# Norm sums with tokens on the partitions, and value products one step later

## The chip, the cores and the metric

The kernel runs on one core of a Trainium2 chip. The metric is the device time of one execution, in microseconds. The engines of a core are TensorE (PE), VectorE (DVE), ScalarE (ACT), GpSimd (POOL) and SyncE (SP), which issues the transfers from memory. They run side by side and wait for each other on semaphores.

## The reference

Two layers of a transformer block work on 256 latent tokens and 256 context tokens of width 1024, in fp32. A layer is a SwiGLU half step, four parallel token mixers (A: differential attention, B: neighbourhood attention, C and D: grouped attention, D with a window and a sink) merged by gates and an output projection, and a second SwiGLU half step. Each of these three sub-layers j = 0, 1, 2 is wrapped the same way:

```
u = rms_norm(h, g_in) * (1 + scale) + shift
y = sublayer(u)
h = h + gate * rms_norm(y, g_out)      # rms_norm(x) = x * rsqrt(mean(x*x) + 1e-6) * g
```

So between two sub-layers there is a seam: the mean square of y over the 1024 features of each token gives the factor r, h becomes h + r\*y, and the mean square of the new h gives the factor R of the next norm. In layer 1 the context tokens are dropped after the mixers' keys and values, so the last seam has 256 tokens and the others 512.

## The kernel before

Features stand on the 128 partitions, in KT = 8 tiles, and tokens on the free axis (T = 512 or 256). PSUM is a tile `ps` of 8 banks of 512 columns. Every large fp32 product is done in three parts: high of the weights by high of the activations (L338), high by low (L339), and low by high (L347). `split_high` (ScalarE, L321) and `split_low` (VectorE, L327) make the two halves of each weight unit, two units ahead.

The order of work is written out by hand for each engine; each stage adds its instructions to every engine's queue in turn. The stages of a sub-layer are `Norm`, then `Hidden` and `Down` or the four `Branch` stages, `Merge` and `Out`. `Down` and `Out` are `Result` stages: for each of the 8 tiles of y, `take` (ScalarE) squares the product, copies it with its gain and squares the scaled value, and `add` (VectorE) sums these and h\*y over the tiles into `ssq`, `energy` and `cross`.

The seam. The mean square of the new h isn't computed from h but from sums that are ready earlier: sum(h\*h) + 2 r sum(h\*y) + r\*r sum(y\*y), with the gain in y. `Norm.tensor` sums `ssq` with the last `sq`, `energy` and `cross` over the partitions by products with a matrix of ones (L558 to L564). With ones as the 128 columns of weights each result stands on all partitions: 128x512 numbers of which every row is the same. Then `root` takes a logarithm and an exponential over 512 columns (L507, L509) for r; VectorE makes the sum above in four wide steps on `ssq` and `power` (L613, L617, L620, L622), with `scale_y(0)` between them; a second `root` gives R. From there a loop over the 8 tiles runs: `tmp` = h\*R (L635), ScalarE applies scale and shift (L582) and makes `u_high` (L586), VectorE makes `u_low` (L608), and adds r\*y to h for the tile after (L600, L604). `Norm.head` on TensorE follows tile by tile with the first six weight units (L649, 96 products). The first norm of the program has no result before it: `statistics` squares h on ScalarE and `sums` (L548) adds on TensorE, amid the modulation products (L373, L390) of the first stage.

The branches. A `Branch` walks over J steps (16 in layer 0, 8 in layer 1), each for 128 queries of a pair of heads: scores (L1155), maximum, exponential, scaling (L1499), `flip` transposes the probabilities (L1165), `keep_probs` copies them to `pt` (L1314), and after two steps `mix(p)` multiplies with the values (L1180); `high_of_out` (L1327) and `low_of_out` (L1505) take the result out. Between these stand the products of gates and of the next branch's projections, spread over points of the steps. In B, C and D `mix` writes one bank, so `mix(p)` waits for `o_done` of the pair before, set by `low_of_out`; the last one, `mix(NP - 1)`, follows the last `flip` after the loop:

```
for j in range(J):
    ... scores(j + early), window_parts(1 + 2 * j)
    if j % 2 == 0 and j:
        mix(j // 2 - 1)
    flip(j)
    self.window_parts(pe, 2 + 2 * j)
mix(NP - 1)
```

Of the kernel before, what the change touches and what calls it, by code (L numbers as in the profile page):

```python
# [23 lines left out]
P = 128  # L24
D = 1024
# [157 lines left out]
def build(nc, tokens, small, cond, weights, mods, na_rows, h_kept, c_kept, out, stop=None):  # L183
# [3 lines left out]
    with ExitStack() as ctx:  # L187
# [26 lines left out]
        rstd = place("rstd", [2, S_ALL], F32, at)  # L214
        ssq = place("ssq", [S_ALL], F32, at + 4 * KB)
# [8 lines left out]
        power = place("power", [S_ALL], F32, at); at += 2 * KB  # L224
# [159 lines left out]
        def mod_turn(pe, g):  # L384

            pe.wait_ge(mod_copied.sem, g + 1)
            if g:
                pe.wait_ge(mod_added.sem, g)
            for c in range(2):
                t = pe.matmul(ps[:, 5, 8 * c:8 * (c + 1)], mod_row[:, c * P:(c + 1) * P], sm("pick"),  # L390
                              start=c == 0, stop=c == 1, skip_group_check=True)
            t.then_inc(mod_turned.sem, 1)

        def mod_add(dve, g):
            dve.wait_ge(mod_turned.sem, g + 1)
            tiles = slice(KT * MOD_ORDER[g], KT * (MOD_ORDER[g] + 1))
            dve.tensor_tensor(mod[:, tiles].rearrange("p (j c) s -> p c j s", c=2), ps[:, 5, 0:2 * KT].rearrange("p (c j s) -> p c j s", c=2, s=2),
# [114 lines left out]
        class Norm(Stage):  # L512
# [3 lines left out]
            def __init__(self, layer, j, T, result):  # L516
# [6 lines left out]
                self.y_root = signals.new("y_rstd", 2 if result else 0)  # L523
                self.power_steps = signals.new("power_steps", 4 if result else 1)
                self.h_root = signals.new("h_rstd", 2)
                self.y_scaled = signals.new("y_scaled", KT if result else 0)
# [4 lines left out]
                self.ready = signals.new("u_ready", KT)  # L531

            def statistics(self, act):
# [7 lines left out]
                root(act, ps[:, 7, 0:T], rstd[:, 1, 0:T], self.h_root, 1.0 / D)  # L541

            def sums(self, pe):
                for k in range(KT):
                    pe.wait_ge(self.squared.sem, self.squared.at(k + 1))
                    if k == 0:
                        pe.wait_ge(ones_set.sem, ones_set.at(1))
                    pe.matmul(ps[:, 7, 0:self.T], ones[:, :], sq[:, k % 2, 0:self.T], start=k == 0, stop=k == KT - 1)\  # L548
                        .then_inc(self.summed.sem, 1)

            def tensor(self, pe):
                if not self.result:
                    return
                r, T = self.result, self.T
                if (self.l, self.j) in ((0, 1), (1, 0)):
                    pe.wait_ge(mod_done.sem, (MOD_UNITS - MOD_FIRST * KT) // (2 if self.l == 0 else 1))
                pe.wait_ge(r.squares.sem, r.squares.at(KT - 1))
                pe.matmul(ps[:, 7, 0:T], ones[:, :], ssq[:, 0:T], start=True, stop=False)  # L558
                pe.wait_ge(r.squared.sem, r.squared.at(KT))
                pe.matmul(ps[:, 7, 0:T], ones[:, :], sq[:, 1, 0:T], start=False, stop=True).then_inc(self.summed.sem, 1)  # L560
                pe.wait_ge(r.energies.sem, r.energies.at(KT))
                pe.matmul(ps[:, 2, 0:T], ones[:, :], energy[:, 0:T], start=True, stop=True).then_inc(self.summed.sem, 1)
                pe.wait_ge(r.crosses.sem, r.crosses.at(KT - 1))
                pe.matmul(ps[:, 3, 0:T], ones[:, :], cross[:, 0:T], start=True, stop=True).then_inc(self.summed.sem, 1)  # L564

            def scalar(self, act):
                T = self.T
                if self.result:
                    act.wait_ge(self.summed.sem, self.summed.at(1))
                    root(act, ps[:, 7, 0:T], rstd[:, 0, 0:T], self.y_root, 1.0 / D)  # L570
                for n in range(self.n0 + AHEAD, self.n0 + HEAD - 2):
                    split_high(act, n)
                if self.result:
                    act.wait_ge(self.power_steps.sem, self.power_steps.at(4))
                    root(act, power[:, 0:T], rstd[:, 1, 0:T], self.h_root, 1.0 / D)
# [14 lines left out]
            def vector(self, dve):  # L590
                T = self.T
# [5 lines left out]
                r, R, steps = rstd[:, 0, 0:T], rstd[:, 1, 0:T], self.power_steps  # L597
# [12 lines left out]
                if self.result:  # L610
                    dve.wait_ge(self.y_root.sem, self.y_root.at(2))
                    dve.wait_ge(self.summed.sem, self.summed.at(2))
                    dve.tensor_tensor(ssq[:, 0:T], ps[:, 2, 0:T], r, ALU.mult).then_inc(steps.sem, 1)  # L613
                    scale_y(0)
                    dve.wait_ge(self.summed.sem, self.summed.at(3))
                    dve.wait_ge(steps.sem, steps.at(1))
                    dve.scalar_tensor_tensor(out=ssq[:, 0:T], in0=ps[:, 3, 0:T], scalar=2.0, in1=ssq[:, 0:T],  # L617
                                             op0=ALU.mult, op1=ALU.add).then_inc(steps.sem, 1)
                    dve.wait_ge(steps.sem, steps.at(2))
                    dve.tensor_tensor(ssq[:, 0:T], ssq[:, 0:T], r, ALU.mult).then_inc(steps.sem, 1)  # L620
                    dve.wait_ge(steps.sem, steps.at(3))
                    dve.tensor_tensor(power[:, 0:T], power[:, 0:T], ssq[:, 0:T], ALU.add).then_inc(steps.sem, 1)  # L622
# [3 lines left out]
                else:  # L626
                    dve.wait_ge(self.summed.sem, self.summed.at(KT))
                    dve.tensor_copy(power[:, 0:T], ps[:, 7, 0:T]).then_inc(steps.sem, 1)
                dve.wait_ge(self.h_root.sem, self.h_root.at(2))
# [122 lines left out]
        class Result(Stage):  # L752
# [4 lines left out]
            def result_signals(self, layer, j):  # L757
# [10 lines left out]
                self.crosses = signals.new("h_times_y_added", crossed and KT - 1)  # L768
# [31 lines left out]
            def add(self, dve, m, b):  # L800
# [17 lines left out]
                dve.tensor_tensor(energy[:, 0:T], energy[:, 0:T], sq_y[:, b, 0:T], ALU.add).then_inc(self.energies.sem, 1)  # L818
                dve.wait_ge(self.crossed.sem, self.crossed.at(m + 1))
                if past(m - 1):  # L820
                    dve.wait_ge(self.crosses.sem, self.crosses.at(m - 1))
                dve.tensor_tensor(cross[:, 0:T], cross[:, 0:T], hy[:, b, 0:T], ALU.add).then_inc(self.crosses.sem, 1)

        class Down(Result):
# [11 lines left out]
            def tensor(self, pe):  # L836
                def two_rows(i, last):
                    for e, unit in enumerate(self.units):
# [8 lines left out]
                        product(pe, n, n0, [(ps[:, r, 0:self.T], [(w, k0 + w) for w in range(DOWN_K[part])])],  # L847
# [73 lines left out]
        class Branch(Stage):  # L921
# [194 lines left out]
            def tensor(self, pe):  # L1116
# [77 lines left out]
                for j in range(J):  # L1194
# [5 lines left out]
                    if j % 2 == 0 and j:  # L1200
                        mix(j // 2 - 1)
# [683 lines left out]
```

## Time and profile before

| | |
|---|---|
| time, median of 3 runs | 2534.37 us (2529.94 to 2536.66) |
| the profiled execution's own time | 2532.3 us |
| its span in the profile | 2530.5 us |
| TensorE busy | 2428.9 us (96%) |
| VectorE busy | 1581.3 us (62%) |
| ScalarE busy | 1064.8 us (42%) |
| mean granted TensorE clock | 0.988 of 2.4 GHz |

The span goes from the first to the last instruction; the time also holds what lies around it. In the rows, times are microseconds and durations of single instructions nanoseconds where a row says mean ns. `<-` after an idle time names what the engine waited for. PEld is the load of weights on TensorE. An fp32 product shows as two passes (x2).

### The profile page before, as it was taken

The page shows a single profiled execution, that of the slowest core. Times are in us where ns is not written, and L with a number is a line of the kernel's source. Part 1 is how long each engine was busy: PE and PEld are TensorE (multiplying, and loading weights), DVE is VectorE, ACT ScalarE, POOL GpSimd, SP SyncE. Part 2 cuts the span into 40 slices and gives each one's busy share as a digit, 9 for nine tenths or more (in the row PEclk, how much of TensorE's full clock was granted, in tenths as well). Part 3 has the DMA queues.
Part 4 walks back from the last instruction along what each step waited for, and adds up shares of the span by engine and source line. Part 5 has one row for each costly group of instructions (what it writes and reads, how often), then busy time and mean ns, then how long its engine had stood idle before and what let it go on. Part 6 is the DMA issues. An engine that isn't in the chain of part 4 may idle for free.

```text
span 2530.5 us, 31850 instructions
## 1 busy us (share of the span) xinstructions
PE 2428.9 (96%) x12584; PEld 1973.4 (78%) x12584; DVE 1581.3 (62%) x2620; ACT 1064.8 (42%) x1842; POOL 27.4 (1%) x43
## 2 busy tenths in 40 slices
PE   6999998999999999989999989999989999988998
PEld 3888886877767676768888868888868788778998
DVE  2798888355455557688887874333355456588654
ACT  5222235355454535462222342222354555556444
POOL 0000000000000000000000000000000000000000
PEclk9999999999999999999999999999999999999999
DMA  5556554321322112225655523322234243233554
GB/s 234 184 207 216 187 178 159 95 76 63 104 71 71 63 67 84 71 88 192 210 206 191 186 99 108 100 99 85 96 113 141 76 142 121 88 125 126 185 178 154
DMA packets 98069, 331.42 MB, mean 131 GB/s; under 512 B 11009, under 2 KB 12033, under 8 KB 97281
## 3 DMA queue, kind: packets, MB, share of 16 engines
q1 hardware_dynamic: 97922, 329.39, 38.4%
q8 instruction: 100, 1.64, 0.3%
q14 instruction: 47, 0.39, 0.0%
HBM read 323.06 MB, written 6.29 MB: 130 GB/s over the span
## 4 chain that ended last, share of the span: by engine, by line
PE 90%; DVE 4%; ACT 3%; issue 1%; DMA 1%; SPq 0%; POOL 0%; DVEq 0%; ACTq 0%
PE ps L347 26%; PE ps L338 24%; PE ps L339 24%; PE ps L649 5%; PE ps L1180 3%; PE ps L1155 3%; PE ps L1165 3%; DVE w_low L327 1%; ACT w_high L321 1%; ACT prob L1304 0%; PE ps L548 0%; DMA mod_first<-in_mods 0%; DVE stat L1464 0%; PE ps L1124 0%; ACT pt L1314 0%
## 5 line engine op out<-in xcount | busy, mean ns | idle before, releaser
L327 DVE TENSOR_TENSOR w_low<-raw,w_high 128x1024 fp32r<-128x1024 f32 (+1 forms) x488 | 551.7, 1136 | 495.3 <-ACT w_high L321 494.5
L321 ACT ACTIVATE w_high<-raw 128x1024 fp32r<-128x1024 f32 (+1 forms) x488 | 481.6, 990 | 762.1 <-DMA raw<-in_weights 761.9
L338 PE MATMUL ps<-u_high,w_high 128*128 128x512 f32 (+1 forms) x2208 | 771.0, 361 | 4.2 <-DVE acc L1421 1.4
L339 PE MATMUL ps<-u_low,w_high 128*128 128x512 f32 (+1 forms) x2208 | 762.6, 357 | 0.0
L347 PE MATMUL ps<-u_high,w_low 128*128 128x512 f32 (+1 forms) x2496 | 542.9, 362 | 4.8 <-DVE w_low L327 4.8
L347 PEld LDWEIGHTS ps<-u_high,w_low 128*128 128x128 f32 x2496 | 422.5, 190 | 91.6 <-issue 19.7
L338 PEld LDWEIGHTS ps<-u_high,w_high 128*128 128x128 f32 x2208 | 418.8, 190 | 89.4 <-issue 17.1
L339 PEld LDWEIGHTS ps<-u_low,w_high 128*128 128x128 f32 x2208 | 418.9, 190 | 58.1
L410 DVE CUSTOM_DVE_ANT_0 ps<-mod_raw,c_all,smalls 128x1024 f32<-128x1024 f32 x256 | 319.5, 1290 | 2.2 <-DMA mod_raw<-in_mods 1.7
L338 PE MATMUL ps<-hid_high,w_high 128*128 128x512 f32 (+1 forms) x704 | 249.0, 362 | 0.0
L339 PE MATMUL ps<-hid_low,w_high 128*128 128x512 f32 (+1 forms) x704 | 249.0, 362 | 0.0
L347 PE MATMUL ps<-hid_high,w_low 128*128 128x512 f32 (+1 forms) x704 | 161.6, 362 | 0.0
L338 PEld LDWEIGHTS ps<-hid_high,w_high 128*128 128x128 f32 x704 | 132.9, 189 | 20.6
L339 PEld LDWEIGHTS ps<-hid_low,w_high 128*128 128x128 f32 x704 | 132.9, 189 | 20.6
L1304 ACT ACTIVATE prob<-ps,stat 128x512 f32<-128x512 f32 (+1 forms) x192 | 116.5, 616 | 54.3 <-DVE stat L1475 54.3
L347 PEld LDWEIGHTS ps<-hid_high,w_low 128*128 128x128 f32 x704 | 122.5, 189 | 20.6
L1314 ACT ACTIVATE pt<-ps 128x1024 f32<-128x1024 f32 (+2 forms) x96 | 76.3, 795 | 145.0 <-PE ps L1165 144.7
L1464 DVE TENSOR_REDUCE stat<-ps 128x2 f32<-128x1024 f32 (+1 forms) x96 | 100.4, 1046 | 45.2 <-PE ps L1155 43.1
L649 PE MATMUL ps<-u_high,w_high 128*128 128x512 f32 (+1 forms) x288 | 89.7, 398 | 37.6 <-ACT u_high L586 37.6
L743 DVE TENSOR_TENSOR hid<-silu_g,ps 128x512 f32<-128x512 f32 (+1 forms) x88 | 54.4, 618 | 98.5 <-PE ps L347 98.2
L1155 PE MATMUL ps<-k_all,q_all 64*128 64x512 f32 (+1 forms) x384 | 93.7, 570 | 6.6 <-ACT prob L1304 6.4
L649 PEld LDWEIGHTS ps<-u_high,w_high 128*128 128x128 f32 x288 | 56.5, 205 | 51.3 <-issue 41.3
(151 smaller groups left out, 2258.5 us busy)
## 6 DMA issues: line engine op xcount, KB each, us to landing
raw<-in_weights SPq DMA_DIRECT2D x360, 512.0 KB, 3.5
mod_raw<-in_mods SPq DMA_DIRECT2D x128, 512.0 KB, 4.2
raw<-in_weights SPq DMA_DIRECT2D x64, 384.0 KB, 3.1
raw<-in_weights SPq DMA_DIRECT2D x64, 320.0 KB, 2.9
mod_first<-in_mods SPq DMA_DIRECT2D x16, 512.0 KB, 13.1
h_kept<-h SPq DMA_DIRECT2D x16, 256.0 KB, 2.0
na_bias<-in_na_rows SPq DMA_DIRECT2D x16, 256.0 KB, 4.0
h<-h_kept SPq DMA_DIRECT2D x2, 2048.0 KB, 8.0
```

The source lines that it names most:

```text
L321: act.activation(w_high[s][:, 0:width], raw[s][:, 0:width], ACT.Copy).then_inc(high_made.sem, 1)
L327: dve.tensor_tensor(w_low[s][:, 0:width], raw[s][:, 0:width], w_high[s][:, 0:width], ALU.subtract).then_inc(low_made.sem, 1)
L338: pe.matmul(o, w_high[s][:, w], x_high(x), start=first and a == 0, stop=False)
L339: pe.matmul(o, w_high[s][:, w], x_low(x), start=False, stop=False)
L347: done = pe.matmul(o, w_low[s][:, w], x_high(x), start=False, stop=last and a == len(terms) - 1)
L410: done = dve.tensor_tensor_reduce(out=ps[:, 4 + 2 * s:6 + 2 * s].rearrange("p a b -> p (a b)"), in0=mod_raw[i % MOD_SLOTS][:, :], in1=c_al ...
L649: pe.matmul(ps[:, banks[e], 0:W], w_high[SLOT_OF[self.n0 + e]][:, k], x[:, k, 0:W], start=k == 0 and x is u_high, stop=False)
L1155: m = pe.matmul(ps[:, self.score_bank(j) + s, 0:nkeys], q_all[rows, t, q:q + P], k_all[rows, kt, key:key + nkeys], start=True, stop=True)
L1165: m = pe.transpose(ps[:, 2 + s, c * P:(c + 1) * P], prob[:, j % 2, s, c * P:(c + 1) * P], ident)
L1304: e = act.activation(prob[:, j % 2, s, 0:nkeys], ps[:, self.score_bank(j) + s, 0:nkeys], ACT.Exp, bias=stat[:, j % 2, 1, s:s + 1], scale=S ...
L1314: act.activation(pt[:, j // 2 % 2, 0:ns, 0:nkeys // P, half], ps[:, 2:2 + ns, 0:nkeys].rearrange("p s (c q) -> p s c q", q=P), ACT.Copy).t ...
L1464: dve.tensor_reduce(stat[:, j % 2, 0], both[:, :, 0:nkeys], AX.X, ALU.max).then_inc(self.maxed.sem, 1)
```

## The change

1. The sums of a seam are turned. The sums' data are now the weights, 128 tokens at a time, and one column of ones moves, so that a result is one number per token, tokens on the partitions: 128x4 numbers instead of 128x512 (128x2 for 256 tokens). Each sum is four products (two for 256 tokens).
2. `ssq` and `cross` without their last tile are summed by `early_sums`, before the last low products of the `Result` stage; the last `sq` and `hy` are added in `Norm.tensor`; VectorE no longer adds the last `hy` to `cross`.
3. Both roots and the four steps of the sum work on 128x4 numbers in `by_token`; `small_root` replaces `root`; a third exponential gives sqrt of the mean square, so that the energy is combined in another form.
4. To bring r and R back to all partitions, ScalarE scales the unit matrix per token block (`on_diagonal`, an activation of 128x128 with a per-partition scale), and TensorE multiplies ones by it (`spread_out`). r and R then stand in PSUM banks 4 and 5, and VectorE reads them there.
5. Only one of two `split_high` stands ahead of the second root, the other behind it.
6. The first norm does the same; its `spread_out` stands in TensorE's queue behind the sums. The modulation's turned rows move from bank 5 to bank 3.
7. In B, C and D `mix(p)` runs at step 2p + 3 instead of 2p + 2, with its copies on ScalarE and VectorE; A and the last pair stay where they are.

```diff
+            def on_diagonal(self, act, which, row, signal):
+                for c in range(self.T // P):
+                    act.activation(diag[:, which, c], ident, ACT.Copy, scale=by_token[:, row, c:c + 1]).then_inc(signal.sem, 1)
+            def spread_out(self, pe, which, signal):
+                for c in range(self.T // P):
+                    pe.wait_ge(signal.sem, signal.at(c + 1))
+                    done = pe.matmul(ps[:, 4 + which, c * P:(c + 1) * P], ones[:, :], diag[:, which, c], start=True, stop=True)
+                done.then_inc(self.spread.sem, 1)
+            def small_root(self, act, of, row, steps):
+                act.activation(by_token[:, row, 0:self.T // P], of, ACT.Ln, scale=1.0 / D, bias=eps[:, 0:1]).then_inc(steps.sem, 1)
+                act.wait_ge(steps.sem, steps.at(1))
+                act.activation(by_token[:, row + 1, 0:self.T // P], by_token[:, row, 0:self.T // P], ACT.Exp, scale=-0.5).then_inc(steps.sem, 1)
...
             def sums(self, pe):
-                    pe.matmul(ps[:, 7, 0:self.T], ones[:, :], sq[:, k % 2, 0:self.T], start=k == 0, stop=k == KT - 1)\
-                        .then_inc(self.summed.sem, 1)
+                    for c in range(self.T // P):
+                        done = pe.matmul(ps[:, 2, c:c + 1], sq[:, k % 2, c * P:(c + 1) * P], ones[:, 0:1], start=k == 0 and c == 0,
+                                         stop=k == KT - 1 and c == self.T // P - 1, skip_group_check=True)
+                    done.then_inc(self.summed.sem, 1)
+                self.spread_out(pe, 1, self.h_diag)
...
             def tensor(self, pe):
+                pe.wait_ge(r.squared.sem, r.squared.at(KT))
+                r.sums_of(pe, sq[:, 1], 2, False, True).then_inc(self.summed.sem, 1)
+                pe.wait_ge(r.crossed.sem, r.crossed.at(KT))
+                r.sums_of(pe, hy[:, 1], 3, False, True).then_inc(self.summed.sem, 1)
...
-                pe.matmul(ps[:, 7, 0:T], ones[:, :], ssq[:, 0:T], start=True, stop=False)
-                pe.wait_ge(r.squared.sem, r.squared.at(KT))
-                pe.matmul(ps[:, 7, 0:T], ones[:, :], sq[:, 1, 0:T], start=False, stop=True).then_inc(self.summed.sem, 1)
                 pe.wait_ge(r.energies.sem, r.energies.at(KT))
-                pe.matmul(ps[:, 2, 0:T], ones[:, :], energy[:, 0:T], start=True, stop=True).then_inc(self.summed.sem, 1)
-                pe.wait_ge(r.crosses.sem, r.crosses.at(KT - 1))
-                pe.matmul(ps[:, 3, 0:T], ones[:, :], cross[:, 0:T], start=True, stop=True).then_inc(self.summed.sem, 1)
+                r.sums_of(pe, energy, 7, True, True).then_inc(self.summed.sem, 1)
+                self.spread_out(pe, 0, self.y_diag)
+                self.spread_out(pe, 1, self.h_diag)
...
+            def sums_of(self, pe, x, bank, first, last):
+                for c in range(self.T // P):
+                    done = pe.matmul(ps[:, bank, c:c + 1], x[:, c * P:(c + 1) * P], ones[:, 0:1], start=first and c == 0,
+                                     stop=last and c == self.T // P - 1, skip_group_check=True)
+                return done
+            def early_sums(self, pe):
+                if self.final:
+                    return
+                pe.wait_ge(self.squares.sem, self.squares.at(KT - 1))
+                self.sums_of(pe, ssq, 2, True, False)
+                pe.wait_ge(self.crosses.sem, self.crosses.at(KT - 2))
+                self.sums_of(pe, cross, 3, True, False)
...
-                    if j % 2 == 0 and j:
-                        mix(j // 2 - 1)
+                    for p in self.mixes(j):
+                        mix(p)
+            def mixes(self, j):
+                after = 2 if self.b == "A" else 3
+                return [p for p in range(self.NP - 1) if 2 * p + after == j]
```

In `Down` and `Out` the last unit's `product` is split into `product_high`, `early_sums`, `product_low`. In `Norm.scalar` and `Norm.vector` the steps follow in this order:

```
ScalarE: small_root(y), Exp(scale=-1) of its logarithm, on_diagonal(y), split_high, small_root(h), on_diagonal(h), split_high, then the loop
VectorE: four steps on 128x4 numbers, wait for the spread y factor, scale_y(0), add_y(0), scale_y(1), wait for the spread h factor, then the loop
```

## Rows read from the trace of the kernel before

**Rows 1.** The page, part 4: chain that ended last, by engine.

```profile
PE 90%; DVE 4%; ACT 3%; issue 1%; DMA 1%; SPq 0%; POOL 0%; DVEq 0%; ACTq 0%
```

**Rows 2.** Waits of TensorE: releaser, us in total, times, longest.

```profile
PE ps L649 <- ACT u_high L586: 37.6, 6, 6.8
```

**Rows 3.** Timeline of the seam from `Out` of layer 0: start, length, engine.

```profile
1103.81 0.69 DVE L822 TENSOR_TENSOR cross<-cross,hy 128x512 f32<-128x512 f32 x1
...
1104.53 1.98 PE L347 MATMUL ps<-a_high,w_low 128*128 128x512 f32 x8
...
1106.55 0.60 ACT L788 ACTIVATE sq<-ps 128x512 f32<-128x512 f32 x1 [2.43 <-PE ps L347]
1107.04 0.83 ACT L790 ACTIVATE y<-ps,post 128x256 f32<-128x256 f32 x2
...
1108.47 0.71 ACT L507 ACTIVATE rstd<-ps,eps 128x512 f32<-128x512 f32 x1
1108.64 0.69 DVE L818 TENSOR_TENSOR energy<-energy,sq_y 128x512 f32<-128x512 f32 x1
...
1109.38 1.12 PE L562 MATMUL ps<-energy,ones 128*128 128x512 f32 x2 [1.06 <-DVE energy L818]
1109.75 1.99 ACT L321 ACTIVATE w_high<-raw 128x1024 fp32r<-128x1024 f32 x2
...
1110.61 0.69 DVE L613 TENSOR_TENSOR ssq<-ps,rstd 128x512 f32<-128x512 f32 x1 [0.53 <-PE ps L562]
...
1113.27 0.69 DVE L622 TENSOR_TENSOR power<-power,ssq 128x512 f32<-128x512 f32 x1
...
1115.46 0.69 DVE L635 TENSOR_TENSOR tmp<-h,rstd 128x512 f32<-128x512 f32 x1 [0.30 <-ACT rstd L509]
...
1118.15 0.77 PE L649 MATMUL ps<-u_high,w_high 128*128 128x512 f32 x1 [6.78 <-ACT u_high L586]
```

**Rows 4.** Windows: length, busy us of PE, PEld, DVE, ACT, POOL, granted clock, DMA.

```profile
965.90:969.30 3.40, 1.50 (x9) 0.71 (x7) 2.71 (x8) 2.28 (x6) 0.00 (x0) 1.00 0.00 0
969.31:972.72 3.41, 3.41 (x13) 3.03 (x13) 2.20 (x8) 1.02 (x1) 0.00 (x0) 0.50 0.00 0
...
423.49:446.99 23.50, 23.50 (x97) 19.31 (x98) 20.33 (x29) 13.51 (x23) 0.00 (x0) 0.93 0.19 70
1118.15:1142.42 24.27, 24.27 (x97) 19.89 (x98) 20.32 (x29) 14.79 (x24) 0.00 (x0) 0.90 0.00 1
```

**Rows 5.** Groups by form: count, busy us, mean ns of one, idle before.

```profile
L1302 ACT ACTIVATE stat<-stat 128x2 f32<-128x2 f32 x24 | 4.8, 199 | 6.3 <-DVE stat L1473 6.3
...
L1276 ACT ACTIVATE v_all<-ps 128x128 f32<-128x128 f32 x16 | 3.2, 281 | 1.9 <-PE ps L1124 1.9
...
L1472 DVE TENSOR_TENSOR stat<-smalls,stat 128x2 f32<-128x2 f32 x24 | 3.9, 162 | 0.8
```

**Rows 6.** Timeline of the last seam of layer 1, with 256 tokens.

```profile
2319.61 0.38 ACT L788 ACTIVATE sq<-ps 128x256 f32<-128x256 f32 x1 [0.82 <-PE ps L347]
...
2325.13 0.42 DVE L635 TENSOR_TENSOR tmp<-h,rstd 128x256 f32<-128x256 f32 x1 [0.41 <-ACT rstd L509]
```

**Rows 7.** Timeline of the start: first sums, turned modulation rows, copy of sums.

```profile
28.45 10.14 PE L548 MATMUL ps<-sq,ones 128*128 128x512 f32 x16 [5.39 <-issue]
...
40.30 0.52 PEld L390 LDWEIGHTS ps<-smalls,mod_row 128*128 128x128 f32 x4 [1.19 <-ACT mod_row L382]
40.30 0.61 PE L390 MATMUL ps<-smalls,mod_row 128*128 128x8 f32 x4 [0.71 <-ACT mod_row L382]
...
47.51 0.68 DVE L628 COPY power<-ps 128x512 f32<-128x512 f32 x1
```

**Rows 8.** Timeline of the end of branch B in layer 0.

```profile
774.03 0.60 ACT L1314 ACTIVATE pt<-ps 128x512 f32<-128x512 f32 x1 [1.87 <-PE ps L1165]
...
774.94 0.42 DVE L1505 TENSOR_TENSOR q_low<-ps,q_high 128x256 fp32r<-128x256 f32 x1 [2.37 <-ACT q_high L1327]
...
778.79 1.08 PE L1180 MATMUL ps<-pt,v_all 128*64 128x256 f32 x8 [0.69 <-ACT pt L1314]
```

More of the change, by code:

```diff
@@ L571, in scalar @@
-                for n in range(self.n0 + AHEAD, self.n0 + HEAD - 2):
-                    split_high(act, n)
+                    self.small_root(act, ps[:, 2, 0:C], 1, self.y_root)
+                    act.activation(by_token[:, 3, 0:C], by_token[:, 1, 0:C], ACT.Exp, scale=-1.0).then_inc(self.y_root.sem, 1)
+                    act.wait_ge(self.y_root.sem, self.y_root.at(2))
+                    self.on_diagonal(act, 0, 2, self.y_diag)
+                split_high(act, self.n0 + AHEAD)
                 if self.result:
@@ L627, in vector @@
                     dve.wait_ge(self.summed.sem, self.summed.at(KT))
-                    dve.tensor_copy(power[:, 0:T], ps[:, 7, 0:T]).then_inc(steps.sem, 1)
-                dve.wait_ge(self.h_root.sem, self.h_root.at(2))
+                    dve.tensor_copy(row(0), ps[:, 2, 0:C]).then_inc(steps.sem, 1)
+                dve.wait_ge(self.spread.sem, self.spread.at(2 if self.result else 1))
                 for k in range(KT):
@@ L846, in two_rows @@
                             pe.wait_ge(self.hidden.ready.sem, self.hidden.ready.at(FT if part == 3 else FT - 1))
-                        product(pe, n, n0, [(ps[:, r, 0:self.T], [(w, k0 + w) for w in range(DOWN_K[part])])],
-                                lambda k: hid_high[:, k, 0:self.T], lambda k: hid_low[:, k, 0:self.T],
-                                first=part == 0, last=part == 3)
+                        outs = [(ps[:, r, 0:self.T], [(w, k0 + w) for w in range(DOWN_K[part])])]
+                        product_high(pe, n, n0, outs, lambda k: hid_high[:, k, 0:self.T], lambda k: hid_low[:, k, 0:self.T], first=part == 0)
+                        if (i, r, part) == (KT // 2 - 1, 1, 3):
+                            self.early_sums(pe)
+                        product_low(pe, n, n0, outs, lambda k: hid_high[:, k, 0:self.T], last=part == 3)
                 self.rows(two_rows)
@@ L1352, in scalar @@
                     keep_probs(j)
-                    if j % 2 == 0 and j:
-                        high_of_out(j // 2 - 1)
+                    for p in self.mixes(j):
+                        high_of_out(p)
                     if b == "A":
@@ L1534, in vector @@
                             sub_low(p)
-                    elif j % 2 == 0 and j:
-                        low_of_out(j // 2 - 1)
+                    else:
+                        for p in self.mixes(j):
+                            low_of_out(p)
                     self.window_splits(dve, split_low, 2 + 2 * j)
@@ L1627, in tensor @@
                     pe.wait_ge(self.freed.sem, self.freed.at(m - 1))
-                    product(pe, n, n, out, lambda k: a_high[:, k, 0:self.T], lambda k: a_low[:, k, 0:self.T])
+                    product_high(pe, n, n, out, lambda k: a_high[:, k, 0:self.T], lambda k: a_low[:, k, 0:self.T])
+                    if m == KT - 1:
+                        self.early_sums(pe)
+                    product_low(pe, n, n, out, lambda k: a_high[:, k, 0:self.T])
             def scalar(self, act):
```

56 lines of the change are left out of this document (33 added, 23 removed).

## The prediction

> **What bounds the kernel now.** I read the page first. TensorE is 90% of the chain that ended last [rows 1]: a microsecond leaves only where TensorE works less or waits less. The table of its waits says where that is. One wait is large, the first product of a norm's head (L649) on `u_high`: 37.6 us in six places, the seams between stages [rows 2]. A small one stands before the last value products of a branch, 0.69 us for `pt` [rows 8]. The change works on both.
>
> The timeline of one seam shows what the 6.8 us are made of [rows 3]. I count from the first Square on ScalarE after the last product of the stage (1106.55), as t = 0. Square to 0.60; the two copies of `y` 0.49 to 1.32; the root starts at 1.92; `energy` is added from 2.09 to 2.78; its sum starts at 2.83; VectorE's wide steps (L613 to L622) end at 7.41; two wide ScalarE steps; `tmp` starts at 8.91; the head's first product at 11.60. From `tmp` on nothing changes but where the factor is read. So the seam is worth what `tmp` comes earlier.
>
> The windows tell what else the seam costs. Over two whole heads the granted clock is 0.93 and 0.90 in the mean, where 0.50 is 1.2 and 1.00 is 2.4 GHz: 96 products in 23.50 and 24.27 us [rows 4]. The products inside the stages start 0.227 us apart (eight in 1.98 us, one of them 0.39 long, [rows 3]), and 96 of them are 21.8 us: 1.7 and 2.5 us per head are lost to the 1.2 GHz level and to small waits.
>
> **The change, part by part.**
>
> *Sums moved ahead of the last low products.* Per seam `early_sums` puts eight fp32 products (four token blocks, `ssq` and `cross`) in front of the last `product_low`, where TensorE has no idle time. Each is two passes with a 128x128 weight load and one column. The nearest row is the product with 8 columns: four loads in 0.52 us, a load alone 0.19, so 0.11 us per pass [rows 7]. Sixteen passes are 1.76 us; with 256 tokens 0.88 us. There are four seams with 512 tokens and one with 256: **+7.9 us**. Bounds: 0 if the loads hid behind the products before them, which the row speaks against since they are back to back, and twice as much at 1.2 GHz. The one sum that goes (`ssq`, L558) ran in idle time and gives nothing. The wait for `cross` costs nothing: its last addition that is still waited for runs 1103.81 to 1104.50, and the low products start at 1104.53 [rows 3], with 0.9 us of passes over `ssq` to come first.
>
> The Trainium skill (TensorE: Matmul & The Clock Gate, Back-to-back issue gap) gives about 81 ns for a load and product of 128 columns in a stream. By it this term would be 5.8 us instead of 7.9. The trace disagrees: its rows give 0.11.
>
> *The shorter chain, 512 tokens, at 2.4 GHz.* Small steps have rows: ScalarE on 2 numbers 0.20, VectorE 0.16 [rows 5]. A root's logarithm takes 0.11 more than a Square of the same size (0.71 against 0.60), for its bias operand: 0.31. A diagonal block is an activation of 128x128, 0.28 [rows 5] plus 0.11 for its scale operand, 0.39; an activation starts 0.11 before the one ahead of it ends (0.49 against 0.60), so 0.28 apart and 1.23 for four. A split is 1.0 (1.99 for two). A hand-over between engines is 0.05 (2.78 to 2.83). Eight passes end 0.77 after their start plus one product's length, 0.28 (four with 8 columns take 0.61, [rows 7], less three times 0.11): 1.05.
> - Sum of `sq` 0.65 to 1.7. `hy` is multiplied from 1.36 to 2.05 and summed 2.1 to 3.1. `energy` 2.98 to 4.0.
> - ScalarE is free at 1.92: logarithm to 2.2, two exponentials to 2.5, diagonal 2.5 to 3.7, one split of weights to 4.65 (it stays in the way of the second root).
> - Spread of the y factor after the energy sum: 3.86 to 4.95.
> - VectorE's four small steps end at 4.4. The second root starts at 4.6, its diagonal at 5.1 to 6.35, the spread ends at 6.8.
> - VectorE: `scale_y(0)` 4.96, `add_y(0)` 5.68, `scale_y(1)` 6.28, `tmp` at 6.9.
>
> `tmp` comes at 6.9 instead of 8.91: 2.0 us, four times: **-8.1 us**. Bounds: nothing, if the passes run at 1.2 GHz (the energy sum and the spread are each 0.9 us longer and follow each other), and -11 us, if a pass takes half of 0.11 (three groups of eight lie one behind the other). With 256 tokens the same steps give: sums 0.43, 1.25 and 1.69, first diagonal to 2.4, the split in between holds the second root to 3.3, the spread ends at 4.9; before it was 5.52 [rows 6]: **-0.6 us**.
>
> So chain and sums moved cancel: -8.7 + 7.9 = **-0.8 us**. The gain is paid with TensorE time just before it.
>
> *Head's clock.* TensorE stands idle before the head for 2.8 us (6.8 to 9.6) instead of 6.8. Whether the clock then stays up isn't in the trace. I take 0, with -8 us as the bound (1.7 to 2.5 per long head).
>
> *First norm.* The 16 passes of `sums` (10.14 us, [rows 7]) become 64 short ones: 64 x 0.11 = 7.0 at 2.4 GHz, 14.1 at 1.2. Before, the first half ran at the low level; mixed it is again about 10. New is that `spread_out` stands in TensorE's queue ahead of the second half of the modulation products: TensorE waits for the logarithm, exponential, diagonal and last spread, 2.2 us. Behind it are the modulation units, `mod_turn`, VectorE's `mod_add`, the first splits and so the head. Back come the 0.71 us that `mod_turn` waited for `mod_row`, and 0.5 of the 0.68 us copy of the sums [rows 7]: **+1.0 us**.
>
> *Value products a step later (B, C, D).* In the middle steps the table of waits has none for them; the 0.69 us are at the ends of branches. There the order is now: value products of the pair before last, last transposes, last value products. These share one bank with the former, so `o_done` must come first, and its copy stands on ScalarE behind the last `pt`. Rows: `pt` starts at 774.03, `q_low` ends at 775.36, so 1.33 us; a plain wait for `pt` is 0.69, of which 0.65 lie behind the start of `pt` [rows 8]. That adds 0.7 us where the last products follow the transposes at once: B and C of layer 0, and D of layer 1. D of layer 0 has wait to spare, about 0; B and C of layer 1 have a unit's high products in between, which hide it. **+2 us**, bounds -1 and +5.
>
> Sum: -0.8 + 0 + 1.0 + 2.0 = +2.2 us on the profiled execution's 2532.3, which lies 2.1 below the median of 2534.37. I forecast **2537 us**. A difference under 0.3% (7.6 us) can't be told from none here.
>
> **Rivals.**
>
> *Slower: the one-column products don't hold the clock.* A seam or the start then has long stretches that are idle for the clock though loads run. For: the first sums of the program are long products, and behind them the modulation products run at full speed; loads with one column leave the array itself nearly empty. Against: nothing shows loads alone. Price: first sums 14.1 instead of 10.1, +4; the modulation products behind them partly at half speed, +2; in the long seams the gain of 2.0 goes, up to +8, and in half of them half of it, +4; the last low product sometimes slow, +1. That is 2537 + 11 = **2548 us**; it decides if two of the seams fall before their spreads. The Trainium skill (TensorE: Matmul & The Clock Gate, Part 4: PE-mode transpose) says that transposes don't count as busy for the gate as other products do; no row shows it for sums of one column. By such a rule this rival would hold.
>
> *Faster: the clock stays up into the heads.* For: the idle stretch shrinks from 6.8 to 2.8 us. Against: at the start of branch D TensorE was busy for 1.50 of 3.40 us at 1.00, and what followed ran at 0.50 [rows 4], so a gap of seam's size isn't needed for a fall. Price: -1.7 to -2.5 per long head, -8: **2529 us**.
>
> *Faster, sums nearly free* because loads hide under the last high products: -5 or more, with a better chain **2526 us**. Rows of the 8-column product speak against it.
>
> *The late value products stall more*, in all six branches: 6 x 0.7 and a step's copy waited for in D, +5: 2541 us, inside the forecast's own range.
>
> **Chances.** Forecast with its stall variant 0.48 (2532 to 2542); clock not held 0.36; clock kept up 0.10; sums free 0.06. A tenth of the cases of the clock not held stays within 7.6 us, and so does half of the clock kept up; sums free is faster. Range for 8 in 10: 2528 to 2549. Faster by over 0.3% 0.11, within 0.57, slower 0.32.
>
> **What would show it.** Right: in the long seams `tmp` about 6.9 us after the first Square, the last low product 1.8 us later behind 16 loads at 0.11 us; the first modulation products after the sums start 2.2 us later; a wait of 1.4 us before the last value products of B and C in layer 0. Wrong: loads at another pace; rows of the seam with a granted clock of 0.50 before the spreads (rival one), or heads of 22 us with 1.00 (rival two). What would break the sum is a wait on TensorE for `cross` before the last low product, or a slower VectorE in the head, which now reads its factor from PSUM (of the wide steps the one that reads PSUM, L613, takes 0.69 like the one that doesn't, L622, [rows 3]).

## The result, and the profile after

The changed kernel takes 2559.62 us (median of 4 runs, 2552.83 to 2560.77), the kernel before 2535.51 beside it (4 runs). The ratio is 1.0099, 95% interval [1.0087, 1.0112]: about 25 us slower, where I had forecast 2 us and a range that ended at 2549. The profiled execution has a span of 2557.7 us against 2530.5, so its ledger has 27.2 us to explain.

The chain and the waits of TensorE answer to [rows 1, 2]. The waits are columns of releaser, us in total, times, longest.

```profile
PE 91%; DVE 4%; ACT 3%; issue 1%; DMA 1%; SPq 0%; POOL 0%; DVEq 0%; ACTq 0%
```

```profile
PE ps L683 <- ACT u_high L618: 19.0, 6, 5.5
...
PE ps L1234 <- DVE q_low L1564: 6.5, 4, 1.9
```

The heads wait half as long as before, 19.0 us and not 37.6, and the kernel is slower: most of the wait was filled with work, not removed. The timeline of the seam from `Out` of layer 0 answers to [rows 3] (start, length, engine).

```profile
1117.21 0.95 PE L863 MATMUL ps<-ones,ssq 128*128 128x1 f32 x8
...
1118.02 1.03 PE L863 MATMUL ps<-ones,cross 128*128 128x1 f32 x8
...
1118.92 2.07 PE L348 MATMUL ps<-a_high,w_low 128*128 128x512 f32 x8
...
1121.02 0.60 ACT L822 ACTIVATE sq<-ps 128x512 f32<-128x512 f32 x1 [4.22 <-PE ps L348]
...
1124.32 1.84 PE L863 MATMUL ps<-ones,energy 128*128 128x1 f32 x8
...
1126.03 3.76 PE L546 MATMUL ps<-diag,ones 128*128 128x128 f32 x16
...
1128.12 0.69 DVE L635 TENSOR_TENSOR y<-y,ps 128x512 f32<-128x512 f32 x1 [1.56 <-PE ps L546]
...
1130.05 0.68 DVE L669 TENSOR_TENSOR tmp<-h,ps 128x512 f32<-128x512 f32 x1
...
1132.73 0.77 PE L683 MATMUL ps<-u_high,w_high 128*128 128x512 f32 x1 [2.94 <-ACT u_high L618]
```

The early sums take 1117.21 to 1118.92, 1.71 us, as forecast. Counted from the first Square (1121.02), `tmp` comes at 9.03, not at the forecast 6.9; before it was 8.91 [rows 3]. In the timelines of all four long seams it comes at 9.35, 9.03, 8.65 and 9.81, where before it came at 8.9 in each. The eight passes of the energy sum take 1.84 us, those of the early sum of `ssq` 0.95: the later ones run at half pace, start to start 0.214 us a pass and not 0.107. The windows say why and answer to [rows 4] (length, busy us of the engines, granted clock, DMA share).

```profile
1123.75:1137.40 13.65, 10.71 (x39) 9.48 (x40) 10.00 (x22) 11.19 (x23) 0.00 (x0) 0.50 0.01 5
1132.73:1156.97 24.24, 24.24 (x97) 19.88 (x98) 20.30 (x29) 14.82 (x24) 0.00 (x0) 0.90 0.00 1
```

TensorE's granted clock is 0.50 (1.2 GHz) from 1123.75 on: over part of the sum of `hy`, the energy sum, the spreads and the first 4.7 us of the head. The head is as long as before (24.24 and 24.27 us). So the stretch at 1.2 GHz still costs the head what it did, and covers most of the seam as well.

The timeline of the start answers to [rows 7].

```profile
27.77 13.79 PE L573 MATMUL ps<-ones,sq 128*128 128x1 f32 x64 [5.39 <-issue]
42.59 2.08 PE L546 MATMUL ps<-diag,ones 128*128 128x128 f32 x8 [1.03 <-ACT diag L540]
44.59 1.94 PE L374 MATMUL ps<-mod_first,c_pad 128*32 128x256 f32 x16
...
59.04 2.04 PE L683 MATMUL ps<-u_high,w_high 128*128 128x512 f32 x4 [5.49 <-ACT u_high L618]
```

All 64 passes of the first sums run at 0.214 us a pass. Before, the first rise of the clock in the trace was at 34.06, inside the sums, whose sixteen wide passes took 10.14 us [rows 7]; here it is at 51.97, at the end of the modulation products. The end of branch B in layer 0 answers to [rows 8].

```profile
782.75 0.50 PE L339 MATMUL ps<-u_high,w_high 128*128 128x512 f32 x1 [0.50 <-ACT proj L1284]
...
789.16 0.60 ACT L1368 ACTIVATE pt<-ps 128x512 f32<-128x512 f32 x1 [5.03 <-PE ps L1219]
...
790.07 0.42 DVE L1564 TENSOR_TENSOR q_low<-ps,q_high 128x256 fp32r<-128x256 f32 x1 [4.67 <-ACT q_high L1381]
...
790.64 1.08 PE L1234 MATMUL ps<-pt,v_all 128*64 128x256 f32 x8 [1.51 <-DVE q_low L1564]
```

The wait of the last value products is 1.51 us and no longer 0.69, and there is a new one of 0.50 us ahead of it. The ledger, by how much later each point is reached in the profile after than in the one before:

| stretch | us later at its end | added here |
|---|---|---|
| start and first head | 7.97 | +8.0 |
| seam 1 and its head | 10.30 | +2.3 |
| mixers of layer 0 | 12.68 | +2.4 |
| seam 2 (`Out` of layer 0) and its head | 14.56 | +1.9 |
| seam 3 and its head | 16.96 | +2.4 |
| seam 4 and its head | 20.39 | +3.4 |
| mixers of layer 1 | 24.27 | +3.9 |
| seam 5 (256 tokens) and its head | 27.46 | +3.2 |
| end of the span | 27.2 | -0.3 |

The mixers of layer 1 end here at the first product behind branch D. Of the +3.2 of seam 5, 1.8 us are lost before the seam begins, during two stretches at 0.50 (from 2301.35 and from 2321.83, 3.41 us each) that the trace before has not.

### The profile page after: what moved, and what is told of

The parts are those of the page before. It is cut to its first block, busy times and chain, and to the rows that moved or that the text cites. A ratio compares the mean times of both kernels' runs of the same rounds, so it can differ in the third digit from the quotient of the medians.

```text
span 2557.7 us, 32416 instructions
## 1 busy us (share of the span) xinstructions
PE 2470.6 (97%) x12852; PEld 2026.6 (79%) x12852; DVE 1570.0 (61%) x2615; ACT 1070.3 (42%) x1887; POOL 27.4 (1%) x43
## 4 chain that ended last, share of the span: by engine, by line
PE 91%; DVE 4%; ACT 3%; issue 1%; DMA 1%; SPq 0%; POOL 0%; DVEq 0%; ACTq 0%
PE ps L348 26%; PE ps L339 24%; PE ps L340 23%; PE ps L683 5%; PE ps L1234 3%; PE ps L1209 3%; PE ps L1219 2%; PE ps L863 1%; DVE w_low L328 1%; ACT w_high L322 1%; ACT prob L1358 1%; PE ps L573 1%; PE ps L1681 1%; DVE stat L1523 0%; PE ps L546 0%
## 5 line engine op out<-in xcount | busy, mean ns | idle before, releaser
L340 PE MATMUL ps<-u_low,w_high 128*128 128x512 f32 (+1 forms) x2208 | 762.4, 357 | 0.0
L339 PEld LDWEIGHTS ps<-u_high,w_high 128*128 128x128 f32 x2208 | 418.7, 190 | 91.1 <-issue 15.7
L683 PE MATMUL ps<-u_low,w_high 128*128 128x512 f32 (+1 forms) x288 | 89.2, 396 | 0.0
```

What stands on the lines that cost most here:

```text
L339: pe.matmul(o, w_high[s][:, w], x_high(x), start=first and a == 0, stop=False)
L340: pe.matmul(o, w_high[s][:, w], x_low(x), start=False, stop=False)
L683: pe.matmul(ps[:, banks[e], 0:W], w_high[SLOT_OF[self.n0 + e]][:, k], x[:, k, 0:W], start=k == 0 and x is u_high, stop=False)
```

## The experiments

Times are medians. The ratio is to the kernel before on the same chip, with its 95% interval; "over before" is the ratio times 2532 us, since the median of before itself differed between the groups of runs (2531.8 to 2535.5).

| kernel | us | ratio | over before |
|---|---|---|---|
| the change | 2559.62 | 1.0099 [1.0087, 1.0112] | +25 |
| 1 value products later, alone | 2538.33 | 1.0022 [1.0012, 1.0032] | +5.6 |
| 2 norms alone, one column | 2551.41 | 1.0073 [1.0061, 1.0085] | +18.5 |
| 3 norms alone, 128 columns | 2536.78 | 1.0015 [1.0007, 1.0024] | +3.8 |
| 4 before, idle time filled | 2524.46 | 0.9965 [0.9953, 0.9977] | -8.9 |
| 5 as 2, first norm with 128 columns | 2543.63 | 1.0042 [1.0029, 1.0056] | +10.6 |
| 6 as 3, early sums behind the last product | 2530.50 | 0.9987 [0.9978, 0.9996] | -3.3 |
| 7 as 3, idle time filled | 2525.28 | 0.9970 [0.9959, 0.9982] | -7.6 |
| 8 as 6, idle time filled | 2517.11 | 0.9939 [0.9927, 0.9952] | -15.4 |
| 9 whole change, 128 columns | 2541.78 | 1.0041 [1.0029, 1.0054] | +10.4 |
| 10 as 1, last moved pair back | 2533.60 | 1.0005 [0.9996, 1.0015] | +1.3 |
| 11 as 8, seams with one column | 2525.07 | 0.9977 [0.9968, 0.9986] | -5.8 |

**1 and 2: the parts apart.** Kernel 1 is the kernel before with `mixes` of the change. Kernel 2 is the change with

```diff
-                after = 2 if self.b == "A" else 3
+                after = 2
```

> The kernel before with one part of the change alone: the value products of branches B, C and D stand one step later in the order; the norms are those of before. The ledger of the two traces puts 1.5 us at B and 1.5 at C of layer 0, 0.2 at B and C of layer 1, 2.1 at D of layer 1 and -0.7 at D of layer 0. Theory (the part costs its own stall at the last value product and nothing else): +3 to +5 us, about 2539. Rival (the stalls come from the norms' changed splits and not from the order): within 1 us of before, 2535 to 2536.

> The kernel after with the value products put back where they were: the norms' part of the change alone. Theory (the norms' one-column sums, and above all the granted clock around them, carry the loss): +19 to +22 us against before, about 2555, with the head of the seam behind the out product of layer 0 still 24.2 us long. Rival (the parts act on each other, the later value products shift the seams into a bad phase of the clock): +8 to +14, 2545 to 2549.

The first came out at +5.6 us, [3.0, 8.1], a little above the +3 to +5 of its theory, the second at +18.5, [15.4, 21.5], a little below its +19 to +22. Their sum, 24.1, is the change's 25 within these intervals: the parts act separately. The rival of 1, and that of 2, fall. In kernel 2 the head behind `Out` of layer 0 is 24.4 us long, as expected, but `tmp` comes at 7.79 there and not at 9.03: where in a seam the clock falls differs from one kernel to the next. In its four long seams `tmp` comes at 8.96, 7.79, 8.42 and 9.81.

**3: the same products, wider.** The norms alone, and every sum moves 128 columns of ones:

```diff
-  done = pe.matmul(ps[:, bank, c:c + 1], x[:, c * P:(c + 1) * P], ones[:, 0:1], ...)
+  done = pe.matmul(ps[:, bank, c * P:c * P + 128], x[:, c * P:(c + 1) * P], ones[:, 0:128], ...)
```

The readers take every 128th element (`ps[:, 2, 0:T:P]`).

> The kernel of the run on the norms alone, but each sum with tokens on the partitions moves all 128 columns of ones and not one: the same products in the same number, the same 128x128 loads, 128 equal columns of results of which one is read. Theory (one-column products leave TensorE's clock low, and products that move 128 columns raise it): the first norm's 64 sums take 7 us and not 13.8, the clock rises near 34 us as before, the head of the first norm starts at 50 to 52 us and not 59, and the whole is 6 to 10 us faster than the norms alone, 2545 to 2549. Rival (the weight loads of 128x128 fp32 are slow by themselves, or activity is counted by loads as well): the sums keep 0.21 us each in the first norm and the time stays within 2 us of the norms alone.

14.7 us come back (18.5 to 3.8), more than the 6 to 10 that I expected, for a product that moves 128 times as many columns as the old one. The start in the timeline of this kernel:

```profile
28.23 9.80 PE L573 MATMUL ps<-ones,sq 128*128 128x128 f32 x64 [5.39 <-issue]
39.05 1.36 PE L546 MATMUL ps<-diag,ones 128*128 128x128 f32 x8 [1.02 <-ACT diag L540]
```

The same 64 passes with the same loads take 9.80 and not 13.79 us, because the clock rises at 32.93, inside the sums. (I had expected 7; that would have needed 2.4 GHz from the first on.) The first head starts at 51.29, only 0.5 us later than before. The seam from `Out` of layer 0, from the same timeline:

```profile
1109.79 0.60 ACT L822 ACTIVATE sq<-ps 128x512 f32<-128x512 f32 x1 [4.25 <-PE ps L348]
...
1112.89 1.06 PE L863 MATMUL ps<-ones,energy 128*128 128x128 f32 x8
...
1114.88 0.69 DVE L635 TENSOR_TENSOR y<-y,ps 128x512 f32<-128x512 f32 x1 [0.53 <-PE ps L546]
...
1116.87 0.69 DVE L669 TENSOR_TENSOR tmp<-h,ps 128x512 f32<-128x512 f32 x1
...
1119.55 0.77 PE L683 MATMUL ps<-u_high,w_high 128*128 128x512 f32 x1 [2.77 <-ACT u_high L618]
```

Eight passes are again 1.06 us, `scale_y(0)` comes at 5.09 and `tmp` at 7.08 from the first Square, where I had forecast 4.96 and 6.9. The other three long seams have the same 7.08; with 256 tokens `tmp` comes at 5.13, where before it was 5.52 [rows 6]. So the chain that I worked out is the chain at 2.4 GHz. The rival, that loads are slow by themselves, falls. The head still begins at 1.2 GHz, as the windows show:

```profile
1118.37:1125.20 6.83, 5.65 (x13) 4.46 (x14) 6.76 (x11) 6.74 (x12) 0.00 (x0) 0.50 0.00 0
1119.55:1144.24 24.69, 24.69 (x97) 20.17 (x98) 20.29 (x29) 14.79 (x24) 0.00 (x0) 0.89 0.00 1
```

**4: the idle time of the kernel before, filled.** Unused products, read by nobody, stand behind the sums of each seam and behind the second `mod_turn`:

```diff
+        def fill(pe, n):
+            for i in range(n):
+                pe.matmul(ps[:, 6, 0:512], ones[:, :], smalls[:, at:at + 512], start=True, stop=True)
...
+                fill(pe, 7 if T == S_ALL else 4)        # Norm.tensor, behind the sum of cross
+                fill(pe, 6)                             # Modulation.tensor, behind mod_turn(pe, 1)
```

> The kernel before with unused fp32 products of ones by 512 columns added where TensorE idles: seven behind the sums in each seam of 512 tokens and four in each of 256, and six behind the second modulation unit's turn at the start; their results are read by nobody. Theory (the idle time of a seam, 6.8 us, is what sets the clock back, and the 6.8 us stretch at half clock that follows costs each head 2 to 2.5 us): the stretches at half clock at the heads of the seams vanish or shorten, each head of 512 tokens lasts 21.8 us and not 24.2, and the whole is 6 to 12 us faster, 2523 to 2529. Rival (the stretch at half clock comes whatever fills the seam, or the fillers delay the head as much as they give back): 2534 to 2538.

8.9 us faster. No seam and no head of this trace has a stretch at 0.50 any more, and its heads of 512 tokens last 22.28 to 22.34 us, against 23.5 to 24.3 before. I had expected 21.8. The head starts as long after the first Square as before (11.61 us), so the unused products don't delay it. The window over the head behind `Out` of layer 0:

```profile
1112.56:1134.85 22.29, 22.29 (x97) 18.17 (x98) 20.32 (x29) 14.79 (x24) 0.00 (x0) 1.00 0.00 1
```

**5: start or seams.** Kernel 2, with the 128 columns in `Norm.sums` alone.

> The norms alone, with 128 columns of ones moved in the 64 sums of the very first norm and nowhere else; the sums of the seams move one column. Theory (the start and the seams each pay their own stretch at half clock): of the 14.6 us between one column and 128 columns everywhere, the start's 5.8 come back here and the seams' 8.7 don't, 2545 to 2547. Rival (the late rise at the start also shifts what comes behind it, and most of the loss goes with it): 2539 to 2542.

Inconclusive: 2543.6 lies between the theory (2545 to 2547) and the rival (2539 to 2542). By the ratios 7.9 us of the 14.7 come back and 6.8 belong to the seams, each uncertain by over 3 us. What the trace shows is the start: the first head starts at 51.42, as in 3 (51.29), and 5.7 us ahead of kernel 2. In its four long seams `tmp` still comes at 9.81, 9.55, 9.13 and 8.31, and not at 7.08. So the seams have a part of their own (kernel 11 shows it better).

**6: the early sums' place.** Kernel 3, without `early_sums` ahead of the last low products:

```diff
                 r = self.result
+                pe.wait_ge(r.squares.sem, r.squares.at(KT - 1))
+                r.sums_of(pe, ssq, 2, True, False)
                 pe.wait_ge(r.squared.sem, r.squared.at(KT))
                 r.sums_of(pe, sq[:, 1], 2, False, True).then_inc(self.summed.sem, 1)
+                pe.wait_ge(r.crosses.sem, r.crosses.at(KT - 2))
+                r.sums_of(pe, cross, 3, True, False)
```

> The kernel with 128 columns in every sum of the norms, but the early sums are taken out from in front of the last low product and stand behind it, the squares' part in front of the last square's sum and the cross part behind it. Theory (the early sums' 1.7 us were on the path, but behind the last product TensorE has only 1.0 us of idle time before the y spread to take them, so its queue of six sums of 0.88 us delays the spread by 1.2 us): 2533 to 2536, 1 to 3 us faster than with early sums. Rival (they vanish wholly in TensorE's idle time): 7.7 us faster, 2529. Rival (they delay the chain by their whole length): no change, 2537.

7.1 us less than 3: my theory of a queue that delays the spread by 1.2 us was wrong, and the first rival nearly right. The profiled execution is the fastest of the eleven (2523.18), so I take only distances inside a seam from it. The timeline of TensorE in the same seam:

```profile
1104.50 1.97 PE L348 MATMUL ps<-a_high,w_low 128*128 128x512 f32 x8
1106.31 1.05 PE L867 MATMUL ps<-ones,ssq 128*128 128x128 f32 x8
1107.20 1.12 PE L867 MATMUL ps<-ones,sq 128*128 128x128 f32 x8
1108.16 1.06 PE L867 MATMUL ps<-ones,cross 128*128 128x128 f32 x8
1109.05 1.06 PE L867 MATMUL ps<-ones,hy 128*128 128x128 f32 x8
1109.94 1.06 PE L867 MATMUL ps<-ones,energy 128*128 128x128 f32 x8
```

The energy sum starts 5.44 us after the last low product here, and 5.23 in 3 (1107.66 to 1112.89). So 1.71 us leave the path and 0.2 come back in each seam: 1.5 times four, 0.8 at 256 tokens, 6.8 us. TensorE had that idle time between the sums of the seam.

**7 and 8: both, with the rest filled.** Fillers as in 4, but three behind the spread of the R factor at 512 tokens, two at 256, six behind the second `mod_turn`, added to 3 and to 6.

> The kernel with 128 columns in every sum of the norms, plus unused fp32 products of ones by 512 columns in the idle time that is left: three behind the spread of the h roots in each seam of 512 tokens, two at 256, six behind the second modulation turn; their results are read by nobody. Theory (idle time ahead of a head is what brings its stretch at half clock): heads of 512 tokens last 22.3 us as in the filled kernel before, and not 23.6 to 24.7, 8 us less in all, 2527 to 2530. Rival (the stretch is set by the few, short products of the sums in front and not by the 2.8 us idle behind them): 2535 to 2538.

> Both of the two kernels above in one: early sums behind the last low product, and the unused products in the idle time in front of each head. Theory (the two gains add): 2524 to 2528, level with or a little slower than the filled kernel before at 2524.5, as the shorter chain of the norms and the extra loads of its sums about cancel. Rival (early sums behind the last product already hold the clock, so the fillers give nothing more): equal to the kernel without fillers, 2533 to 2536.

Both rivals fall: the kernels take 11.4 and 12.1 us less than without fillers. Both theories named the right effects and were too careful with them: 7 lies 2 us under its range (8 us less, 2527 to 2530), 8 lies 7 us under its own (2524 to 2528). Heads of 512 tokens last 22.3 us in 7, as expected. Kernel 8 is the fastest of all, 0.6% under the kernel before. It isn't level with kernel 4, as I had expected, but 6.6 us ahead of it: where the clock is held in both, the head starts 10.08 us after the first Square in 8 and 11.61 in 4, in each of the four long seams. So the shorter chain is worth its 1.5 us a seam once its sums cost no time on the path and hold the clock. The whole seam and its head run at 2.4 GHz in its windows:

```profile
1111.49:1133.90 22.41, 22.41 (x98) 18.27 (x99) 20.30 (x29) 14.80 (x24) 0.00 (x0) 1.00 0.00 1
1101.20:1111.50 10.30, 9.54 (x64) 7.58 (x62) 6.79 (x16) 9.28 (x24) 0.00 (x0) 1.00 0.15 52
```

**11: one column again.** Kernel 8, with the sums of the seams back at one column and the fillers kept.

> The kernel with early sums behind the last low product and the unused products, but the sums of the seams move one column again; the first norm keeps 128 columns. Theory (short one-column sums lower the clock by themselves, whatever fills the rest): stretches at half clock come back at the heads, 6 to 12 us slower than with 128 columns, 2523 to 2529. Rival (with the idle time filled, the sums' columns don't matter): within 2 us of it, 2515 to 2519.

9.6 us of 15.4 are lost again, as the theory had it, and the rival falls. The timeline of TensorE in the seam from `Out` of layer 0:

```profile
1103.57 0.95 PE L875 MATMUL ps<-ones,ssq 128*128 128x1 f32 x8
1104.42 1.05 PE L875 MATMUL ps<-ones,sq 128*128 128x1 f32 x8
1105.34 1.03 PE L875 MATMUL ps<-ones,cross 128*128 128x1 f32 x8
1106.23 1.37 PE L875 MATMUL ps<-ones,hy 128*128 128x1 f32 x8
1107.46 1.85 PE L875 MATMUL ps<-ones,energy 128*128 128x1 f32 x8
1109.16 3.76 PE L553 MATMUL ps<-diag,ones 128*128 128x128 f32 x16
```

and its windows:

```profile
1103.57:1106.76 3.19, 3.19 (x30) 3.19 (x29) 1.54 (x4) 2.96 (x10) 0.00 (x0) 1.00 0.46 167
1106.76:1113.59 6.83, 6.83 (x31) 6.31 (x31) 2.94 (x8) 4.44 (x11) 0.00 (x0) 0.50 0.00 0
```

TensorE is busy without a gap from the last products of `Out` on, and the clock still falls, at 1106.76, in the middle of the sums. Idle time can't be blamed for that: with 128 columns in the same place, kernel 8 stays at 1.00. What I had expected wrongly is where the loss shows. The stretches at 0.50 lie over the sums and the unused products and end before the long heads, which last 22.3 us at 1.00 as in 8. What is lost is the chain: the long heads start 11.58, 12.09, 11.77 and 11.19 us after the first Square and not 10.08, and with 256 tokens 7.81 and not 6.84, in all 7.3 of the 9.6 us.

**9: the whole change with 128 columns.**

> The whole change, with 128 columns of ones moved in every sum of the norms in place of one. Theory (the parts add: norms with 128 columns 4.1 us over before, later value products 5.6): 2541 to 2545, so some 15 to 17 us of the change's 25 over before come back by the columns alone. Rival (the value products' stall depends on where the norms put the branches, it was 8 us between the norms alone and the whole): 2545 to 2549.

2541.8 us, at the lower end of the theory and outside the rival, +10.4 where the parts' sum is 9.4: some 15 us of the change's 25 come back by the columns alone.

**10: the stall of the value products.** Kernel 1, with the last moved pair of each branch where it was:

```diff
-                return [p for p in range(self.NP - 1) if 2 * p + after == j]
+                return [p for p in range(self.NP - 1) if 2 * p + (2 if p == self.NP - 2 else after) == j]
```

> The kernel before with the later value products, except for the last pair but one of each branch, which stays where it was, so that only the last pair stands behind the loop as before. Theory (the loss is the 1.5 us wait of the last value products for their low part, as two pairs' splits stand directly behind each other, and the 0.5 us wait behind the last flip): both waits vanish, 2531 to 2535. Rival (every value product pays for standing a step later): 2537 to 2539.

+1.3 us, [-1.0, 3.8], not to be told from zero: the theory holds and the rival falls. No cost of the middle products is seen; the loss is at the end of the branch. Waits of TensorE in kernel 1:

```profile
PE ps L1180 <- DVE q_low L1510: 6.5, 4, 1.9
...
PE ps L338 <- ACT proj L1230: 1.7, 3, 0.7
```

and in kernel 10:

```profile
PE ps L1180 <- ACT pt L1314: 3.6, 5, 1.1
...
PE ps L338 <- ACT proj L1230: 0.7, 1, 0.7
```

## Why the prediction was wrong, point by point

**The step that failed** is the term "The shorter chain, 512 tokens, at 2.4 GHz", -8.1 us, and with it "mixed it is again about 10" in the first norm. Both took the clock of the kernel before for granted, while the change took out the wide products during which it had been high. At 2.4 GHz the chain is right (`tmp` at 7.08 in kernel 3, forecast 6.9). In the changed kernel the clock is at 0.50 over most of the sums and spreads of the seams, and `tmp` comes at 9.35, 9.03, 8.65 and 9.81 against 8.91: +1.2 us instead of -8.1. The first norm was put at +1.0 and measured +8.0 in the ledger: 13.79 us of sums, a spread of 2.08, and modulation products of 1.94 and 5.02 us where kernel 3 has 9.80, 1.36, 1.07 and 2.80. The term "Head's clock", taken as 0, was nearly right: the four long heads of the change are 1.7 us longer together than before.

**Early sums, +7.9:** right in size (1.71 us a seam; 7.1 by kernel 6, after the 0.2 us that come back).

**256 tokens, -0.6:** somewhat too large. At 2.4 GHz it is -0.4 (5.13 in kernel 3 against 5.52); in the change `tmp` comes at 5.48 and the gain is gone here too.

**Value products, +2:** the place and the mechanism were right, the size was not. I had the longer wait for `q_low` (1.51 us against the forecast 1.4, 0.82 more than before where I had 0.7), and missed a second one, 0.50 us more, of the high products behind a branch's last flip but one, on ScalarE's copy of a projection or a gate. That is 1.3 us in each of B and C of layer 0 and D of layer 1, 4.0 in all, less 0.5 that D of layer 0 gains. The places of the same products in the traces of kernel 1 and of before give about 4 in all: B falls 1.5 us further behind, C 1.5, layer 1's mixers 1.5, and D of layer 0 gains 0.5. A further 1.1 us are lost while kernel 1 runs through a stretch at 0.50 from 2299.05 that before lacks. The whole, about 5, agrees with the times (5.6 [3.0, 8.1]). What brings that stretch stays open: kernel 3 has one there too, without moved value products.

**Rival one was the truth and under-priced.** I gave it 0.36, for the doubt that "nothing shows loads alone". Its start was well priced (4 + 2 beside the forecast's 1.0; measured 8.0). Its seams were not: I let half of them lose half of their gain, and over the four of them the whole gain of 7.3 us went, and 1.2 more. The Trainium skill (TensorE: Matmul & The Clock Gate, Part 4: PE-mode transpose) says of transposes that they don't count as busy in the way other products do; kernels 3 and 11 show a like thing of one-column products, worth 14.7 and 9.6 us. Its mechanism was written down, and I kept the forecast on the clock as before.

**Rival two** (clock kept up into the heads, 2.8 us idle) did not hold: in kernel 3 the idle time is 2.77 us and the head still has 5.65 us at 0.50. The price that I gave a held head, 1.7 to 2.5 us, was a little high: a head of 22.3 us in kernels 4 and 7 is 1.2 to 2.0 us shorter than one of before, and 1.3 to 2.4 shorter than one of kernel 3. **Rival three** (sums free under the high products) falls: 0.107 us a pass, as forecast. **The fourth**, value products that stall more, priced at +5, came nearest of all to its own measurement (+5.6), but by other waits than "in all six branches".

| term | forecast | measured, from |
|---|---|---|
| early sums | +7.9 | +7.1 (6 against 3) |
| chain of five seams at 2.4 GHz | -8.7 | -7.7 ((8.91 - 7.08) x 4 and 5.52 - 5.13, traces of before and 3) |
| first norm at its forecast clock | +1.0 | +0.5 (start of the first head, 51.29 against 50.78, traces of 3 and before) |
| low clock with one column | 0 | +14.7 (2 against 3) |
| value products | +2 | +5.6 (1) |

These rows add up to +20.2 of the change's 25. Most of the rest is in kernel 3 already: by its rows it should be at +7.1 - 7.7 + 0.5 = -0.1, and it measured +3.8 [1.8, 6.1]. Its trace has two stretches at 0.50 in layer 1 (from 2149.19 and from 2299.38, 3.41 us each) that before lacks. Over the first the same products fall about 1.3 us further behind those of before, over the second 1.1, so these two hold 2.4 of the 3.9 us. What brings them isn't shown, and the other 1.5 us stay open.

## What to carry to other kernels

Before a wide product is made narrow, ask what it does besides its result: here the wide sums were what TensorE ran while its clock stayed high, and the wide ones were the cheaper by 14.7 us. A shorter wait is worth its length only if what fills it isn't new work on the same engine; here the same sums cost 7 us ahead of the last product and nearly nothing behind it. And where TensorE idles ahead of its heaviest products, look at the granted clock of what follows: here it was worth filling that time with products that nobody reads.

## What the runs showed of the hardware

- With a 128x128 load in fp32, a pass takes 0.107 us at 2.4 GHz for 1 moved column (sixteen in 1.71 us, the change) and for 128 (sixteen in 1.70 us, kernel 3). So the wider product cost nothing in its own time.
- At 1.2 GHz such a pass takes 0.214 us (64 in 13.79).
- In kernel 11 TensorE was busy without a gap and its granted clock still fell to 0.50, in the middle of sums of one column; with 128 columns in their place it stayed at 1.00 (kernel 8).
- An idle time of 2.77 us ahead of a head was followed by 5.65 us of that head at 0.50 (kernel 3); filled down to 0.20 us, the head ran at 1.00 throughout (kernel 7).
- Unused products in idle time gave 8.9 us to the kernel before and 12.1 to kernel 6 (0.35% and 0.48%).
